# First block's attention taken two batches at a time on all engines, sliding heads' scores on 64 rows each

## What is computed

```python
def swa_sink_attention(q, k, v, sinks, rel_bias):        # 8 query heads, 2 key/value heads
    s_w = einsum('bnqhgd,bnkhd->bhgnqk', qr, kw) * scale + b_w   # own block of 128 and the one before
    s_w = where(valid_w, s_w, NEG_INF)
    s_m = einsum('bnqhgd,bmhd->bhgnqm', qr, km) * scale + b_m    # 16 meta tokens
    p = softmax_with_sink(concatenate([s_m, s_w]), sink)
    o = einsum(p[..., :N_META], vm) + einsum(p[..., N_META:], vw)

def forgetting_attention(q, k, v, f_logit):              # 8 heads, causal over all tokens
    sb = einsum('bqhd,bkhd->bhqk', q_blk, k) * scale + c_blk[..., None] - cum[:, :, None, :]
    pb = softmax(where(k_pos <= q_pos, sb, NEG_INF))
    o = einsum('bhqk,bkhd->bqhd', pb, v)

mix = concatenate([o_a, o_b]); h = h + rms_norm(mix @ w_out)     # then the feed-forward part
```

## Time and profile before

| | |
|---|---|
| median of 3 runs | 1752.8 us (1751.95 to 1752.92) |
| the profiled execution's own time | 1753.0 us |
| its span | 1751.0 us |
| PE busy | 1709.7 us, 98% of the span |
| DVE / ACT / POOL busy | 61% / 39% / 7% |
| granted TensorE clock, mean | 0.987 |
| attention of the first block | from 112 to 256 us in the span |

### The profile page before, as it was taken

The page is one execution under the profiler, slowest core; times in us unless marked ns, Lnnn a source line. Parts: engine busy times, 40 slices in busy tenths (PEclk is TensorE's granted clock), DMA queues, the critical chain, the costliest instruction groups (busy, mean ns, idle before and its releaser), DMA issues.

```text
span 1751.0 us, 20420 instructions
## 1 busy us (share of the span) xinstructions
PE 1709.7 (98%) x8190; PEld 1386.1 (79%) x8190; DVE 1066.8 (61%) x1729; ACT 691.2 (39%) x1055; POOL 117.4 (7%) x114
## 2 busy tenths in 40 slices
PE   8999999999999999999899999999999899999996
PEld 8877777888888887878688888887878688888885
DVE  7446547766664346644479765667645368867565
ACT  4445654322222244565423222532565522332532
POOL 2100000110000000100000000021100000000012
PEclk9999999999999999999999999999999999999998
DMA  4321012655554221212122222221322122222221
GB/s 174 138 84 49 25 49 85 216 195 194 196 194 158 99 96 67 103 72 73 49 96 97 97 96 97 91 89 53 113 89 73 49 73 98 97 97 97 93 96 48
DMA packets 29532, 177.40 MB, mean 101 GB/s; under 512 B 3613, under 2 KB 3757, under 8 KB 12286
## 3 DMA queue, kind: packets, MB, share of 16 engines
q1 hardware_dynamic: 20448, 144.71, 22.8%
q0 software_dynamic: 8608, 31.21, 5.1%
q10 hardware_dynamic: 382, 0.19, 0.0%
HBM read 171.28 MB, written 4.78 MB: 101 GB/s over the span
## 4 chain that ended last, share of the span: by engine, by line
PE 77%; DVE 5%; issue 2%; ACT 1%; DMA 0%; DVEq 0%; ACTq 0%
PE ps L612 24%; PE ps L614 24%; PE ps L613 24%; PE ps L1129 1%; PE ps L1111 1%; DVE h L1664 1%; PE ps L1117 1%; DVE ps L2076 1%; ACT w_hi L1209 1%; PE ps L650 0%; ACT Pc L1209 0%; PE ps L1198 0%; DVE w_lo L1664 0%; DVE cacc L1671 0%; DMA w_raw<-in_w 0%
## 5 line engine op out<-in xcount | busy, mean ns | idle before, releaser
L612 PE MATMUL ps<-Xh,w_hi 128*128 128x512 f32 (+1 forms) x1664 | 652.9, 392 | 4.8 <-DVE Xl L1664 3.4
L614 PE MATMUL ps<-Xh,w_lo 128*128 128x512 f32 (+1 forms) x1664 | 638.4, 384 | 0.0
L613 PE MATMUL ps<-Xl,w_hi 128*128 128x512 f32 (+1 forms) x1664 | 638.2, 384 | 0.0
L1664 DVE TENSOR_TENSOR w_lo<-w_raw,w_hi 128x2048 fp32r<-128x2048 f32 (+1 forms) x158 | 311.6, 1975 | 248.3 <-ACT w_hi L1209 248.1
L1209 ACT ACTIVATE w_hi<-w_raw 128x2048 fp32r<-128x2048 f32 (+1 forms) x152 | 259.3, 1709 | 297.4 <-DMA w_raw<-in_w 275.6
L612 PEld LDWEIGHTS ps<-Xh,w_hi 128*128 128x128 f32 x1664 | 312.7, 188 | 77.4 <-issue 15.5
L613 PEld LDWEIGHTS ps<-Xl,w_hi 128*128 128x128 f32 x1664 | 312.7, 188 | 65.1 <-issue 5.5
L614 PEld LDWEIGHTS ps<-Xh,w_lo 128*128 128x128 f32 x1664 | 312.5, 188 | 62.2
L1671 DVE SCALAR_TENSOR_TENSOR cacc<-ain,vec,cacc 128x512 f32<-128x512 f32 x240 | 161.9, 745 | 0.0
L1209 ACT ACTIVATE gt<-ps 128x512 f32<-128x512 f32 x48 | 28.6, 597 | 194.3 <-PE ps L614 194.3
L1209 ACT ACT_TABLE_LOAD x54 | 69.3, 1283 | 4.0 <-issue 3.0
(11 more groups left out here) (306 smaller groups left out, 2069.5 us busy)
## 6 DMA issues: line engine op xcount, KB each, us to landing
w_raw<-in_w SPq DMA_DIRECT2D x134, 1024.0 KB, 4.8
ada_w<-in_w_ada POOLq DMA_DIRECT2D x48, 512.0 KB, 4.7
bias_scratch<-brow POOLq DMA_DIRECT2D x2, 1312.0 KB, 5.9
h<-in_xT SPq DMA_DIRECT2D x4, 512.0 KB, 5.9
out<-h SPq DMA_DIRECT2D x4, 512.0 KB, 2.6
bias<-bias_scratch POOLq DMA_DIRECT2D x1, 1024.0 KB, 9.2
bias<-bias_scratch POOLq DMA_DIRECT2D x1, 512.0 KB, 4.7
cact<-in_c POOLq DMA_DIRECT2D x1, 512.0 KB, 6.6
```

Source lines behind the costliest of these rows:

```text
L612: nc.tensor.matmul(o_, whi, xhi, start=start, stop=False)
L613: nc.tensor.matmul(o_, whi, xlo, start=False, stop=False)
L614: return nc.tensor.matmul(o_, wlo, xhi, start=False, stop=stop)
L1664: return nc.vector.tensor_tensor(o_, a_, b_, op)
```

## The change

All three loops go by pairs. PE: `scores` of both batches of pair 0, then for every pair both `transposes`, two dense steps (`MID_STEPS`), `scores` of the next pair, `values`, and the pair's other dense steps. ACT: both `turned_copy`, what belongs to the even batch (`after_batch`), both `exps` of the next pair, what belongs to the odd batch, and at even p `out_hi`. DVE: both `normed`, both `maxima` of the next pair, the `slot_lo` of the pair before, and at even p `out_lo`. `scores(p)` waits for `pt_done` of both batches of the pair before.

The sliding heads' scores are written by `window_scores`: for each piece of keys one matmul on partitions 0 to 63 (even batch) and one on 64 to 127 (odd batch), in turn. There is one buffer `Ka` with both key heads, without zeros; ACT fills it in two copies of 128 partitions instead of four of 64, and POOL clears two pads less.

```diff
-FIRST_STEPS = 7
+FIRST_STEPS, MID_STEPS = 7, 2
+PAIRS = BATCHES // 2
 def dense_until(j):
-    return FIRST_STEPS + -(-(j + 1) * (DENSE_STEPS - FIRST_STEPS) // BATCHES)
+    def after_pair(p):
+        return FIRST_STEPS + -(-(p + 1) * (DENSE_STEPS - FIRST_STEPS) // PAIRS)
+    if j % 2 or j == BATCHES - 2:
+        return after_pair(j // 2)
+    return after_pair(j // 2 - 1) + MID_STEPS
-        Ka = [sb_at("Ka0", [P, NM + T], F32, o_ka), sb("Ka1", [P, NM + T])]
+        Ka = sb_at("Ka", [P, NM + T], F32, o_ka)
+            def window_scores(p):
+                i = (p - PAIRS // 2) // 2
+                units = batch_columns(2 * p)
+                for u, (b, n, c0, _) in enumerate(units):
+                    pieces = [(c0, slice(0, n))] if b < 2 else \
+                        [(c0, slice(0, NM)), (c0 + NM, slice(NM + P * (b - 1), NM + P * (b + 1)))]
+                    for c, keys in pieces:
+                        for e in range(2):
+                            r = slice(DH * e, DH * (e + 1))
+                            last = nc.tensor.matmul(buffer(2 * p + e, c, keys.stop - keys.start),
+                                                    Qa[r, i, b * P:(b + 1) * P], Ka[r, keys], start=True, stop=True)
+                            if u == 1 and c != c0 or u == 1 and len(pieces) == 1:
+                                last.then_inc(s_full, 1)
             # PE
-            for j in range(BATCHES):
-                transposes(j)
-                dense(dense_until(j))
-                if j + 2 < BATCHES:
-                    scores(j + 2)
-                if j == BATCHES - 1:
+            for p in range(PAIRS):
+                transposes(2 * p)
+                transposes(2 * p + 1)
+                dense(dense_until(2 * p))
+                if p + 1 < PAIRS:
+                    scores(p + 1)
+                else:
                     split_ready(S_OW)
                     window_step(0, (0, 1))
                     window_step(1, (0, 1))
-                if j % 2:
-                    values(j)
+                values(2 * p + 1)
+                dense(dense_until(2 * p + 1))
             # ACT
+            exps(0)
+            exps(1)
+            for p in range(PAIRS):
+                turned_copy(2 * p)
+                turned_copy(2 * p + 1)
+                after_batch(2 * p)
+                if p + 1 < PAIRS:
+                    exps(2 * p + 2)
+                    exps(2 * p + 3)
+                after_batch(2 * p + 1)
+                if p % 2 == 0 and p:
+                    out_hi(p // 2 - 1)
             # DVE
+            for p in range(PAIRS):
+                normed(2 * p)
+                normed(2 * p + 1)
...
+                if p + 1 < PAIRS:
+                    maxima(2 * p + 2)
+                    maxima(2 * p + 3)
+                for j in (2 * p - 2, 2 * p - 1):
+                    if j in SPLITS:
+                        slot_lo(*SPLITS[j])
+                if p % 2 == 0 and p > 1:
+                    out_lo(p // 2 - 1)
+            slot_lo(*SPLITS[BATCHES - 2])
             out_lo(7)
```

More of the change, by code:

```diff
@@ L511, in _ @@
             pool.dma_start(vec1[:, :], a["vec1"]).then_inc(first_in, 16)
-            for i, pad in enumerate((Vm[:, :], PTm[:, :, :], Ka[0][DH:P, :], Ka[1][0:DH, :], Kb[DH:P, :, :])):
+            for i, pad in enumerate((Vm[:, :], PTm[:, :, :], Kb[DH:P, :, :])):
                 if i:
@@ L829, in scores @@
+            def scores(p):
+                if p:
+                    pe.wait_ge(pt_done, 2 * p)
+                if p == 2:
                     pe.wait_ge(bank_read[1], q1_fill)
-                if j == FOX_BATCHES // 2:
+                if p == PAIRS // 4:
                     for b in range(2):
                         pe.wait_ge(bank_read[b], q2_fills[b])
-                if j >= FOX_BATCHES and j % 4 == 0:
-                    i = (j - FOX_BATCHES) // 4
+                if p >= PAIRS // 2 and p % 2 == 0:
+                    i = (p - PAIRS // 2) // 2
@@ L835, in scores @@
                     pe.wait_ge(bank_read[i % 2], qa_fills[i])
-                (fox_scores if j < FOX_BATCHES else swa_scores)(j).then_inc(s_full, 1)
+                if p < PAIRS // 2:
+                    for j in (2 * p, 2 * p + 1):
+                        fox_scores(j).then_inc(s_full, 1)
+                else:
+                    window_scores(p)
             def transposes(j):
@@ L916, in window_step @@
                         last.then_inc(slot_done if j == 3 else tile_full, 1)
-            pe.wait_ge(pads_zero, 5)
+            pe.wait_ge(pads_zero, 3)
             pe.wait_ge(cum_done, 2)
@@ L924, in _ @@
             scores(0)
-            scores(1)
             dense(dense_until(-1))
-            for j in range(BATCHES):
-                transposes(j)
-                dense(dense_until(j))
-                if j + 2 < BATCHES:
-                    scores(j + 2)
-                if j == BATCHES - 1:
+            for p in range(PAIRS):
[4 more added lines that the diff above has]
+                    scores(p + 1)
+                else:
                     split_ready(S_OW)
@@ L1285, in _ @@
             full(tf, 0, False)
[L1286 to L1291, removed]
+            sc.wait_ge(pads_zero, 3)
+            act_(Ka[:, 0:HALF], bank(0, HALF), ACT.Copy)
+            act_(Ka[:, HALF:2 * HALF], bank(1, HALF), ACT.Copy).then_inc(bank_read[0], 1)
             full(tf, 0, True)
@@ L1394, in _, with after_batch @@
             act_(warm[:, :], eps[:, 0:1], ACT.Exp)
[L1395 to L1402, removed]
+            def after_batch(j):
                 for t in tiles_ended(j):
@@ L1406, in _ @@
                     slot_hi(*SPLITS[j])
-                if j % 4 == 0 and j:
-                    out_hi(j // 4 - 1)
+            exps(0)
[10 more added lines that the diff above has]
+                    out_hi(p // 2 - 1)
             out_hi(7)
@@ L1773, in _ @@
             ve.wait_ge(va_turned, 1)
-            ve.wait_ge(pads_zero, 5)
+            ve.wait_ge(pads_zero, 3)
             nc.vector.tensor_copy(V[:, :, 0:P], bank(4).rearrange("p (k q) -> p k q", k=NB))
@@ L1863, in _ @@
             maxima(0)
-            for j in range(BATCHES):
-                normed(j)
-                if j + 1 == FOX_BATCHES:
+            maxima(1)
+            for p in range(PAIRS):
+                normed(2 * p)
+                normed(2 * p + 1)
+                if p + 1 == PAIRS // 2:
                     ve.wait_ge(bias_in, 64)
                     ve.wait_ge(nsink_done, 1)
[L1869 to L1874, removed]
+                if p + 1 < PAIRS:
[7 more added lines that the diff above has]
+            slot_lo(*SPLITS[BATCHES - 2])
             out_lo(7)
```

## The result

The changed kernel takes **1777.0 us** (median of 4 runs, 1773.9 to 1777.3), beside 1752.9 of the kernel before (median of 4): ratio 1.0134, 95% interval 1.012 to 1.0149. Slower by 24 us; 1775 was forecast. The profiled execution was the fastest of the four: 1773.88 us, span 1772.1, mean granted clock 0.984.

A forecast was written before the change was run, and what follows sets the result against it. PE was taken to bound the kernel, with DVE and ACT in its shadow. Scores -7, switches +1, order +23 and clock +5 gave +22 us on 1753.0: 1775 us, range 1765 to 1786.

The forecast's parts named there:

- The order (+23): In the attention, PE waits for `normed`, held behind DVE's low part awaiting ACT's high part; gaps together +23 us.
- second gaps: PE waits ahead of the odd batch's transposes, for its `normed`, after each long gap: seven of 0.4 us, 2.8 together.
- The sliding scores (-7): On PE, a pair's two heads on different rows share the array, cutting 16.0 us of scores to 9.2: -7 us.
- The ratio of 1.74: Sharing gain assumed for sliding scores: 0.84 ns a column for unshared scores against 0.48 for the values' shared matmuls.
- Switches (+1): On PE, one more step between kinds of matmul per sliding pair, eight times 0.11 us: +1 us, between 0 and +3.
- The clock (+5): PE's clock falls to 1.2 GHz after four of seven gaps, 1.3 us each: +5 us, between 0 and +14.
- The key buffer (0): Four copies of 0.38 us become two, beside PE's matmuls at 31 to 33 us: price 0, gain 0.8 at most.
- the clock holds: Rival: PE's gaps come in the attention but no clock fall follows; +17 us, 1770; chance 0.20.
- falls at nearly every gap: Rival: the clock falls at nearly every attention gap, about 2 us each; 1784 us; chance 0.12.
- the heads share nothing: Rival: sliding scores on 64 rows share nothing on PE, so the 7 us are not saved; 1782; chance 0.11.
- the chain keeps up: Rival: `normed` is not held behind the low part, gaps come to 4 us, full sharing; -3 us, 1750; chance 0.05.

The follow-up runs named there:

- e_lo_late: Changed kernel with only DVE's `out_lo` moved, from behind an even pair's maxima to behind both `normed` of the next, odd pair; 1754.0 us, ratio 1.0009.
- e_hi_early: Changed kernel with only ACT's `out_hi` moved, ahead of an even pair's turned copies instead of behind the next pair's exponentials; 1757.8 us, ratio 1.0033.
- e_lo_twice: Changed kernel with each of DVE's seven low parts ahead of a `normed` written twice, same values; 1781.5 us, ratio 1.0159.
- e_before_rows64: Kernel before, in its own order, with one key buffer and each head's sliding scores on its 64 rows, one head at a time; 1756.4 us, ratio 1.0017.
- the best reordering: Changed kernel with DVE's `out_lo` and `slot_lo` behind both `normed`, and one dense step moved between a sliding pair's transposes; 1751.0 us, ratio 0.9988.
- e_rows128: Changed kernel in its own order, sliding scores over all 128 rows with two zero-padded key buffers, heads still in turn; 1780.2 us, ratio 1.016.

## Why the prediction was right

**The order (+23): right in place and size.** Gaps of 2.0, 2.0, 1.5, 3.1, 2.6, 2.7 and 3.5 us were worked out ahead of batches 6, 10, ... 30; the profile has 1.80, 1.78, 1.29, 3.11, 2.60, 2.63 and 3.35, together 16.6 for 17.4. The stations agree too: from e, the end of the scores at 143.43, PE was ready at e + 3.3, fox_h ended at e + 3.3 (e + 3.4 computed) and `normed` of batch 6 began at e + 4.0 (e + 4.1). In a sliding pair (e at 200.53) the transposes came at e + 6.7, as computed. The pairs without a low part (batches 20, 24, 28) have 0.63, 0.30 and 0.64 and two second gaps of 0.16, 1.9 us for 2.8. The 0.4 us ahead of the odd transposes mostly show not as idle but as longer transposes: those of a forgetting pair behind a gap take 1.69 us for 1.44 elsewhere. Longer rows come to about 5.5 us in all, twice the 2.8 that the walk had for second gaps. Most of this belongs to the order by pairs and not to the low part: in e_lo_late, without the long gaps, the transposes are still 2.8 and the dense steps 2.1 us longer than before. Two sums on paper were off by 0.1: DVE is free at e + 2.4 by its own terms, and the sliding gap is 6.7 - 3.5 = 3.2. The walk along DVE's queue is what e_lo_late, e_hi_early and e_lo_twice confirm: take the low part away from in front of `normed` and the long gaps go, let it start at once and a third stays, double it and each grows by its length.

**The sliding scores (-7): right by luck on PE, and half of it in time.** 17.1 us (16.0 in the prediction, which took the step behind the scores off) became 9.7 at full clock, -7.4. The ratio of 1.74 that I took from the values was too low: a pair takes the time of one head, so the sharing is complete; but a head on 64 rows takes 0.1 to 0.2 us more than on 128 (e_before_rows64), which I had not priced, and the two errors met by luck. The Trainium skill ("TensorE: Matmul & The Clock Gate", on small-K matmuls) has the full half, and the trace agrees once the form's own price is taken out. What I did not see is that the chain behind the scores would swallow half of what they save: "what a faster score saves in such a pair still counts" holds only by half. On 128 rows the even head's maxima start 0.43 us earlier, counted from the end of the pair's scores, and the rows of 64 give that up. In the sum this loss lies within the gaps and the longer rows.

**Switches (+1): right.** The dense step ahead of 64-row scores takes 1.57 us for 1.48, eight times, 0.7 us. The drain at a change of tiling mode of the Trainium skill ("TensorEngine Tiling (Array Packing)", key properties) may be what costs the 0.09 us there, and the 0.1 to 0.2 us more that a head on 64 rows takes; no run separates it from other causes.

**The clock (+5): right in size, its two factors not.** Three falls in place of four, and 1.5 us each in place of 1.3. From the stretches above they cost at most 4 x (0.43 + 0.42 + 0.22 + 0.20) = 5.1 us; comparing each with the same rows at full clock gives 1.6, 1.5 and 1.5, 4.6 together. The three runs without a profile were 3 us longer at a mean clock of 0.982 to 0.983 for 0.984; one or two more falls would do that (e_lo_twice, with five, has 0.983), but those runs have no trace, so it is not shown.

**The key buffer (0): right.** Two copies of 0.39 us at 31 us, nobody waiting.

The sum: idle 18.3, lengthened rows about 5.5 (what is left over), falls 4.6, switches 0.8, scores -7.4, 21.8 in the attention. Of the rivals, "the clock holds" (1770) was wrong by the three falls; "falls at nearly every gap" (1784) did not happen here, though e_lo_twice with longer gaps came near it (five falls, 1781.5); "the heads share nothing" was refuted by 0.90 and 1.51 us a pair; "the chain keeps up" failed at its own criterion, `normed` of batch 6 before e + 2: the scores ended at 143.4 and it began at 147.4, e + 4.0. That its time, 1750, is nearly what the best reordering reaches (1751.0) is chance.

## What to carry to other kernels

When a loop is regrouped, look for hand-overs that stood one step apart on two engines: the consumer kept its place in the queue, the producer moved behind new work, and what stands behind the consumer pays. Walk the queue of each engine with durations from the trace, and put whatever nobody awaits soon (low parts, weight splits) behind what the bounding engine waits for. And before paying for a gain on the bounding engine with a coarser order, see what cover it leaves: with all of a pair's batches in the same phase the chain of one no longer hides behind the other, and here most of a real 7 us went that way.

## What was not expected of the hardware

- A matmul group on 64 rows is dearer alone than one of 128 rows with zeros: 0.90 against 0.70 to 0.80 us and 1.50 against 1.31 to 1.41 a batch, with 0.09 more on the step ahead; the second head on the other 64 rows is then free.
- Whether heads must stand in turn depends on the pieces: 0.91 us out of turn against 0.90 for two matmuls a head, 2.27 against 1.51 for four.
- Of the changed kernel's, e_rows128's and e_lo_twice's long gaps, 12 of the 14 from 2.16 to 4.08 us came with a fall to 1.2 GHz, and none of the seven from 1.28 to 2.02 us. Eight of the falls began after the gap's end and four shortly before it. In e_lo_twice a gap of 2.53 us was followed by one and a gap of 2.51 us was not, so the length of the gap alone does not decide. What does stays open.
